# A chunked delta-rule recurrence on 64x64 squares in place of block-diagonal 128x128 matrices, with its vectors loaded early

## The chip, the cores and the metric

The kernel runs on one core of one Trainium2 chip. Its time is the device time in microseconds (us). TensorE (PE) multiplies and writes to PSUM; VectorE (DVE), ScalarE (ACT) and GpSimd (POOL) work beside it; SyncE (SP) issues most transfers. The four compute engines and SP run by themselves and wait for one another by semaphores. The kernel before took 2236.09 us (median of three runs, 2231.66 to 2236.36).

## The reference

The program is a two-layer block (retention, RG-LRU, two feed-forward layers), then a mixing layer over 256 context and 256 sequence tokens, then a product-key feed-forward layer. The change is in the mixing layer alone. What matters of it is its recurrence, of 4 heads with 64x64 states, in both directions of time, over 512 tokens:

```python
def step(S, inp):
    r_t, kk_t, v_t, w_t, b_t, k_t = inp
    sa = jnp.einsum('bhij,bhj->bhi', S, kk_t)
    S = S * w_t[:, :, None, :] - sa[..., None] * b_t[:, :, None, :] + v_t[..., None] * k_t[:, :, None, :]
    return S, jnp.einsum('bhij,bhj->bhi', S, r_t)
...
w_raw = w0 + jnp.einsum('btdr,drc->btdc', lw, w_up)          # tokens x 2 directions x 256 columns
decay = jnp.exp(-jnp.exp(-jax.nn.softplus(-w_raw) - 0.5))
a = jax.nn.sigmoid(a0 + jnp.einsum('btdr,drc->btdc', la, a_up))
kk = (k * k_k).reshape(B, T, RW_H, RW_DH)                    # then scaled to unit length
```

Beside it the layer has a neighbourhood attention of 8 heads (scores, a table of relative positions that is masked by column, softmax, output) and a short convolution; the three results go through one output projection.

## The kernel before, in words

The mixing layer first projects the tokens (`MIX_SLOTS`: seven slots of up to 512 columns of one weight matrix, each loaded by SP, split into a high part by ACT, L1076, and a low part by DVE, L1555, and multiplied in three products each, L2293 to L2295). `MIX_UNITS` says which piece of which slot goes to which tensor; slot 3 holds the gate and most of the attention's queries, slots 4 and 5 its keys and values and the convolution's columns, slot 6 the rest of the convolution.

After the last slot PE waits for vectors and low-rank weights (SP's loads at L887 to L896, issued behind a wait until slots 5 and 6 are used, since they lie in memory that those slots' parts occupied), computes eight `decay` units (L2572), DVE adds the bias (L1889), ACT takes the sigmoid (L1364), and DVE makes the scaled keys (L1892 to L1914). Only then does the recurrence start.

The recurrence works in chunks of 64 tokens, two to a tile of 128 rows, in four steps k with two directions d each: forward takes the tiles 0, 1, 2, 3, backward 1, 0, 3, 2. Each step makes cumulative decays (`cum`, L2663), scaled keys (L1975 to L1980), transposes (`tr`, L2674), products within the chunk (`ab`, and `l` where outputs are wanted, L2686), a product with v (`bv`, L2692), the inverse of a triangular matrix by five doublings (`lev`, L2697, then for n = 1 to 5 `t`, L2701, a transpose of the inverse so far; `y`, L2705, the level's part of A times it; `xy`, L2711, the product that is subtracted), `ug` (L2717), `mn` (L2725 to L2729: how the chunk maps a state), `rt` (L2740 to L2747) and, for each chunk, `st` (L2647 to L2656), which takes the state on. All are fp32. Each matrix is a 128x128 block for a pair of chunks or of heads, whose off-diagonal 64x64 quarters are zero, made so by masks on DVE (`MASK`, 16 masks of 128 columns). PSUM banks are evicted by ACT (`t`, `y`, `tr`, `ug`) and DVE (`xy`, `mn`, `lev`).

The order on all engines is one list, `RW_PLAN` (L254): the recurrence's units with d = 0 and d = 1 in turn, and at every 13th place a piece of an attention head (`ns` scores, `nt` a transposition, `no` output). Four PSUM banks go round (`unit`, L296); every engine works strictly in the order of its own instructions. POOL masks the attention's table (L1042), SP loads it (L881).

Within one unit, four products of 128x128 stand one behind another, for example `xy`:

```python
for j in range(4):
    ins = nc.tensor.matmul(quarter(j), TI[d][:, j // 2, j % 2, :], YY[d][:, j // 2, j % 2, :], start=True, stop=True)
```

Of the kernel before, what the change touches and what calls it, by code (L numbers as in the profile page):

```python
# [21 lines left out]
ALU = mybir.AluOpType  # L22
# [6 lines left out]
P = 128  # L29
D = 1024  # L30
# [14 lines left out]
def host_constants():  # L45
# [15 lines left out]
    same = a // 64 == b // 64  # L61
    for d in range(2):
        after = (lambda u, v: u > v) if d == 0 else (lambda u, v: u < v)
        for n in range(6):
            m = 1 << n

            out[f"level{d}{n}"] = ((a // (2 * m) == b // (2 * m)) & (a // m != b // m) & after(a, b)).astype(f4)
        out[f"strict{d}"] = (same & after(b, a)).astype(f4)
        out[f"incl{d}"] = (same & (after(b, a) | (a == b))).astype(f4)
    out["same"] = same.astype(f4)  # L70
# [6 lines left out]
    out["colok"] = ok.astype(f4)  # L77
# [122 lines left out]
def lru_size(kind, n):  # L200
# [7 lines left out]
MIX_SLOTS = [(1536, 512), (0, 512), (512, 512), (1024, 512), (2048, 512), (2560, 512), (3072, 384)]  # L208
# [11 lines left out]
    (3, [("t", 0, SEQ)], ("g", 0)), (3, [("t", 128, SEQ), ("t", 256, SEQ)], ("q", 0)), (3, [("t", 384, SEQ)], ("q", 2)),  # L220
    (4, [("t", 0, CTX), ("t", 0, SEQ)], ("nk", 3)),
    *[(4, [("n", t, 128, 384)], ("nv", t)) for t in range(4)],
    (5, [("n", t, 0, 128) for t in range(4)], ("nv3", 0)),
    (5, [("t", 128, SEQ), ("t", 256, SEQ)], ("z", 0)), (5, [("t", 384, SEQ)], ("z", 2)),
    (6, [("t", 0, SEQ), ("t", 128, SEQ)], ("z", 3)), (6, [("t", 256, SEQ)], ("z", 5)),
]


def rwkv_plan():


    st = lambda k, n: [(k, d, k ^ d, "st", n) for d in range(2)] if k >= 0 else []
    for k in range(4):
        work = ([("cum", 0), ("tr", 0), ("tr", 1), ("ab", 0), ("ab", 1)] + [("l", 0), ("l", 1)] * (k >= 2)
                + [("bv", 0), ("lev", 0)])
        for n in range(1, 6):
            work += [("t", n), ("y", n), ("xy", n)]
        work += [("ug", 0), ("mn", 0), ("mn", 1)] + [("rt", 0)] * (k >= 2)
        for what, n in work:
            for d in range(2):  # L240
                yield k, d, k ^ d, what, n
# [8 lines left out]
OTHER_WORK = {4: ("cv", 0), 6: ("cv", 1), 70: ("cv", 2), 72: ("rg", 0), 74: ("rg", 1)}  # L250
NO_UNIT = ("st", "nm", "nx", "no", "ny", "cv", "rg")
# [41 lines left out]
RB = 3  # L293

# [153 lines left out]
def first_and_second_block(nc, A, consts, out, mods, upto=99):  # L448
    cols = lambda name: consts[:, CONST_AT[name][0]:sum(CONST_AT[name])]
    with ExitStack() as ctx:  # L450
# [100 lines left out]
        CL = stage.take("context_lo", [P, KT, S], F32R)  # L551
        XC = stage.take("context", [P, TT, D])
        AB = stage.take("ada_bias", [P, 4, BANK])
        again = Region("split context", split_at, stage.end - split_at)
        WA = again.take("decay_and_a", [P, 4, 2, 2, 256])
        NP = Region("k, before", again.at, 8 * KB).take("scaled", [P, TT, D])
        KD = again.take("rw_k", [P, 4, 512])
        CKM = again.take("na_columns", [P, 2, 64])
        FLIP = again.take("na_flip", [P, P])
        GAIN = [XC[:, 0, :], Region("attention output, later", again.at, 4 * KB).take("gain", [P, D])[:, :]]  # L560
        NY = again.take("na_y", [P, TT, 512])
        RW2 = again.take("rw_y2", [P, TT, 256])
# [14 lines left out]
        AA = [ring.take(f"a_raw{d}", [P, 2, 2, P]) for d in range(2)]  # L577
        XX = [ring.take(f"inv_t{d}", [P, 2, 2, P]) for d in range(2)]
        TI = [ring.take(f"inv{d}", [P, 2, 2, P]) for d in range(2)]
        BT = [ring.take(f"b_t{d}", [P, 2, 2, P]) for d in range(2)]  # L580
        LL = [xs_again.take(f"l_t{d}", [P, 2, 2, 2, P]) for d in range(2)]
        AM = [scratch.take(f"a_level{d}", [P, 2, 2, P]) for d in range(2)]
        YY = [scratch.take(f"a_x{d}", [P, 2, 2, P]) for d in range(2)]
        NUG = [scratch.take(f"minus_u_g{d}", [P, 2, 4, 64]) for d in range(2)]
        hh_again = Region("idle input", hh_at, 8 * KB)
        MN = [hh_again.take(f"m_n{d}", [P, 2, 4, P]) for d in range(2)]
        EP = AM
        EN = YY
        RTt = [ring.take(f"r_turned{d}", [P, 2, P]) for d in range(2)]
        SB = [ring.take(f"state{d}", [P, 2, P]) for d in range(2)]  # L590
# [184 lines left out]
        def _(sp):  # L775
# [86 lines left out]

            for j, (c0, n) in enumerate(MIX_SLOTS):
# [3 lines left out]
                for h in range(2):  # L867
                    sp.dma_start(dst[:, 4 * h:4 * h + 4, :], W["w_in_2"][:, 4 * h:4 * h + 4, c0:c0 + n])\
                        .then_inc(s_wload[r], 16)
            deep(SLOTS["mix_out"], W["w_out_2"], 4)  # L870
            r, use = slot(SLOTS["mix_out"] + 1)
            sp.wait_ge(s_wlo[r], use)
            sp.dma_start(CKM[:, 0, :], cols("colok")).then_inc(s_bias, 16)
            sp.dma_start(CKM[:, 1, :], cols("colno")).then_inc(s_bias, 16)
# [8 lines left out]
            for j in range(2):  # L883
                r, use = slot(SLOTS["mix_in"] + 5 + j)
                sp.wait_ge(s_wused[r], use + 1)
            for n, (name, d) in enumerate([("rw_w0_2", 0), ("rw_a0_2", 0), ("rw_w0_2", 1), ("rw_a0_2", 1)]):
                sp.dma_start(RWR[:, n * 256:(n + 1) * 256], A[name][0, d].partition_broadcast(P)).then_inc(s_mix, 16)  # L887
            for n, name in enumerate(["rw_k_k_2", "rw_k_a_2", "rw_r_k_2", "rw_lnx_g_2"]):
                src = A[name][0].rearrange("h j -> (h j)") if name == "rw_r_k_2" else A[name][0]
                sp.dma_start(RWR[:, (4 + n) * 256:(5 + n) * 256], src.partition_broadcast(P)).then_inc(s_mix, 16)  # L890
            sp.dma_start(LORA[:, 0, :], A["rw_w_up_2"][0].rearrange("d r c -> (d r) c")).then_inc(s_mix, 16)
            sp.dma_start(LORA[:, 1, :], A["rw_a_up_2"][0].rearrange("d r c -> (d r) c")).then_inc(s_mix, 16)
            sp.dma_start(LORA[:, 2, :], A["rw_g_up_2"][0]).then_inc(s_mix, 16)
            sp.dma_start(chk, cols("chunk")).then_inc(s_mix, 16)
            sp.dma_start(prow[:, :], cols("same")).then_inc(s_mix, 16)
            sp.dma_start(MASK[:, :, :], consts[:, CONST_AT["level00"][0]:CONST_AT["same"][0]]  # L896
                         .rearrange("p (m n) -> p m n", n=P)).then_inc(s_mask, 16)
# [50 lines left out]
        def _(pool):  # L948
# [87 lines left out]
            for qt in range(TT):  # L1036
                if qt == 0:
                    pool.wait_ge(s_bias, 16 * 19)
                table = BIAS[:, qt, :, :].rearrange("p h (r c) -> p (h r) c", c=64)
                for j, op in enumerate((ALU.mult, ALU.add)):  # L1040
                    mask = CKM[:, j:j + 1, :].broadcast_to([P, 32, 64])
                    ins = nc.gpsimd.tensor_tensor(table, table, mask, op)  # L1042
                    if j == 0:
                        chain.done(ins)
# [1863 lines left out]
```

## Time and profile before

| | |
|---|---|
| median of three runs | 2236.09 us (2231.66 to 2236.36) |
| the profiled execution | 2229.75 us, span 2227.9 us |
| PE busy | 2033.6 us, 91% of the span |
| DVE busy | 1437.3 us, 65% |
| ACT busy | 1054.9 us, 47% |
| POOL busy | 407.8 us, 18% |
| granted TensorE clock, mean | 0.963 |
| stretch of the recurrence, 998 to 1283 us | PE busy 269.06 of 285 us, DVE 126.67, ACT 96.02 |

The busy share of PE is that of pipelined matmuls whose ends are modelled, so it is read beside the distance between their starts. In the trace an fp32 matmul shows as two records of a weight load (PEld) and two of a matmul (PE), an fp32 transpose as one of each. "128*64" in a row is the size of the part of the array that an instruction uses (rows * columns of weights), and the number behind it the size of what streams through.

### The profile page before, as it was taken

How to read it: one execution, taken by the hardware profiler on the slowest of the kernel's cores; microseconds unless marked ns; L12 is line 12 of the kernel's file. 1: busy time of each engine (PE TensorE's matmuls, PEld its weight loads, DVE VectorE, ACT ScalarE, POOL GpSimd, SP SyncE). 2: the span in 40 equal slices, each digit the busy share in tenths (PEclk: the TensorE clock that was granted, in tenths of full speed). 3: DMA queues.
4: the chain of work that ended last, by engine and by line, in shares of the span. 5: the costliest groups of instructions: out<-in, count | busy, mean ns of one | idle time of the engine just before them, and what ended most of it. 6: DMA issues, size and time to landing. Idle time of an engine off the chain costs nothing.

```text
span 2227.9 us, 36659 instructions
## 1 busy us (share of the span) xinstructions
PE 2033.6 (91%) x13383; PEld 1821.8 (82%) x13383; DVE 1437.3 (65%) x2240; ACT 1054.9 (47%) x2062; POOL 407.8 (18%) x333
## 2 busy tenths in 40 slices
PE   6998899987989999969999958988899999999996
PEld 6876788877888888958888848988899998777775
DVE  5536677767767664243544475888799995666665
ACT  4343444357654444323333343444477775555554
POOL 2101000001000000030000000777766672000000
PEclk9999999998999999978999979999999999999998
DMA  7552466744457863220000163555544444555553
GB/s 257 189 189 85 166 234 221 249 161 142 170 189 235 270 232 134 85 68 1 1 1 1 39 151 81 152 156 155 170 140 139 139 143 165 190 190 189 188 188 132
DMA packets 212850, 333.64 MB, mean 150 GB/s; under 512 B 23654, under 2 KB 141148, under 8 KB 212584
## 3 DMA queue, kind: packets, MB, share of 16 engines
q1 hardware_dynamic: 209320, 321.20, 44.9%
q0 software_dynamic: 3392, 10.52, 1.3%
q8 instruction: 96, 1.57, 0.3%
q14 instruction: 42, 0.34, 0.0%
HBM read 330.58 MB, written 1.08 MB: 149 GB/s over the span
## 4 chain that ended last, share of the span: by engine, by line
PE 65%; DVE 13%; PEld 7%; DMA 5%; issue 4%; ACT 3%; SPq 2%; PEldq 1%; DVEq 0%; POOL 0%; ACTq 0%
PE psum L2293 17%; PE psum L2295 16%; PE psum L2294 16%; DMA u_rows<-in_peer_u_dram 3%; PE psum L2865 3%; PEld psum L2293 2%; PEld psum L2294 2%; PEld psum L2295 2%; DVE u_turned L2196 2%; PE psum L2705 2%; DVE weights_lo L1555 2%; PE psum L2711 2%; SPq L921 2%; PE psum L2686 1%; ACT weights_hi L1076 1%
## 5 line engine op out<-in xcount | busy, mean ns | idle before, releaser
L1555 DVE TENSOR_TENSOR weights_lo<-weights,weights_hi 128x1024 fp32r<-128x1024 f32 (+2 forms) x336 | 345.5, 1086 | 261.7 <-ACT weights_hi L1076 256.4
L2293 PE MATMUL psum<-input_hi,weights_hi 128*128 128x256 f32 x1288 | 371.3, 288 | 14.5 <-issue 5.3
L1076 ACT ACTIVATE weights_hi<-weights 128x1024 fp32r<-128x1024 f32 (+2 forms) x336 | 289.3, 931 | 178.6 <-PEq L2340 118.6
L1055 POOL TENSOR_TENSOR u_lo<-u_turned,u_hi 128x512 fp32r<-128x512 f32 x256 | 329.9, 1311 | 217.2 <-ACT u_hi L1452 217.2
L2294 PE MATMUL psum<-input_lo,weights_hi 128*128 128x256 f32 x1288 | 367.3, 285 | 0.0
L2295 PE MATMUL psum<-input_hi,weights_lo 128*128 128x256 f32 x1288 | 367.0, 285 | 0.0
L2293 PE MATMUL psum<-input_hi,u_hi 128*128 128x256 f32 x1024 | 298.8, 292 | 14.0 <-POOL u_lo L1055 13.0
L2294 PE MATMUL psum<-input_lo,u_hi 128*128 128x256 f32 x1024 | 292.1, 285 | 0.0
L2295 PE MATMUL psum<-input_hi,u_lo 128*128 128x256 f32 x1024 | 292.0, 285 | 0.0
L2293 PEld LDWEIGHTS psum<-input_hi,weights_hi 128*128 128x128 f32 x1288 | 249.8, 194 | 29.8 <-issue 28.0
L2294 PEld LDWEIGHTS psum<-input_lo,weights_hi 128*128 128x128 f32 x1288 | 249.9, 194 | 0.0
L2295 PEld LDWEIGHTS psum<-input_hi,weights_lo 128*128 128x128 f32 x1288 | 249.7, 194 | 0.0
L2293 PEld LDWEIGHTS psum<-input_hi,u_hi 128*128 128x128 f32 x1024 | 198.3, 194 | 16.5 <-issue 11.1
L2293 PE MATMUL psum<-v_hi,act_hi 128*128 128x512 f32 x512 | 203.7, 398 | 0.0
L2295 PE MATMUL psum<-v_hi,act_lo 128*128 128x512 f32 x512 | 200.5, 392 | 0.0
L2294 PE MATMUL psum<-v_lo,act_hi 128*128 128x512 f32 x512 | 200.0, 391 | 0.0
L2294 PEld LDWEIGHTS psum<-input_lo,u_hi 128*128 128x128 f32 x1024 | 198.7, 194 | 0.0
L2295 PEld LDWEIGHTS psum<-input_hi,u_lo 128*128 128x128 f32 x1024 | 198.4, 194 | 0.0
L2196 DVE STREAM_TRANSPOSE u_turned<-u_rows 128x1024 f32<-128x1024 f32 x128 | 157.9, 1236 | 38.5 <-DMA u_rows<-in_peer_u_dram 33.6
L1452 ACT ACTIVATE u_hi<-u_turned 128x512 fp32r<-128x512 f32 x256 | 147.1, 627 | 12.2 <-DVE u_turned L2196 12.1
L2267 DVE TENSOR_TENSOR act_lo<-act_table,act_hi 128x256 fp32r<-128x256 f32 x128 | 54.5, 425 | 133.6 <-ACT act_hi L1527 133.6
L1527 ACT ACTIVATE act_hi<-act_table 128x256 fp32r (+1 forms) x128 | 53.5, 418 | 166.3 <-PE psum L2295 166.0
(387 smaller groups left out, 3927.6 us busy)
## 6 DMA issues: line engine op xcount, KB each, us to landing
u_rows<-in_peer_u_dram SPq DMA_DIRECT2D x512, 128.0 KB, 2.7
weights<-in_ffn_w_in_dram SPq DMA_DIRECT2D x44, 1024.0 KB, 7.5
v_rows_even<-in_peer_v_dram SPq DMA_DIRECT2D x64, 512.0 KB, 3.3
v_rows_odd<-in_peer_v_dram SPq DMA_DIRECT2D x64, 512.0 KB, 3.3
weights<-in_ret_w_in_dram SPq DMA_DIRECT2D x24, 1024.0 KB, 7.3
ada_rows_in<-in_ada_w_dram SPq DMA_DIRECT2D x24, 1024.0 KB, 5.4
weights<-in_ffn_w_out_dram SPq DMA_DIRECT2D x44, 512.0 KB, 6.6
weights<-in_lru_w_in_dram SPq DMA_DIRECT2D x12, 1024.0 KB, 6.2
```

What stands on the lines that cost most here:

```text
L921: sp.dma_start(UR[32 * a:32 * a + 32, b, :].rearrange("p (c k) -> p c k", c=4), columns.rearrange("(c e) k -> e c k", c=4)).then_inc(s_ur[ ...
L1055: nc.gpsimd.tensor_tensor(UTL[:, b, half, :], turned[:, half, :], UTH[:, b, half, :].bitcast(F32), ALU.subtract).then_inc(s_ul[b], 1)
L1076: nc.scalar.activation(whi[:, r, at_], wraw[:, r, at_], ACT.Copy).then_inc(s_whi[r], 1)
L1452: nc.scalar.activation(UTH[:, b, half, :], turned[:, half, :], ACT.Copy).then_inc(s_uh[b], 1)
L1527: nc.scalar.activation(AH[:, j % 2:j % 2 + 1, :], GT[:, bass.ds(4 * i + j, 1), :], ACT.Copy)\
L1555: ins = nc.vector.tensor_tensor(wlo[:, r, at_], wraw[:, r, at_], whi[:, r, at_].bitcast(F32), ALU.subtract)
L2196: nc.vector.transpose(UT[j % 4].rearrange("p k (c e) -> p c k e", c=4), UR[:, b, :].rearrange("p (c k j) -> p c k j", c=4, k=KT)).then_inc ...
L2267: nc.vector.tensor_tensor(AL[:, b:b + 1, :], GT[:, bass.ds(4 * i + j, 1), :], AH[:, b:b + 1, :].bitcast(F32), ALU.subtract).then_inc(s_as, 1)
L2293: nc.tensor.matmul(o, ah, bh, start=start, stop=False)
L2294: nc.tensor.matmul(o, ah, bl, start=False, stop=False)
L2295: return nc.tensor.matmul(o, al, bh, start=False, stop=stop)
L2865: ins = nc.tensor.matmul(PS[:, 4 + g % 4, x * P:(x + 1) * P], ONE[:, g % 2, 1, x, :], ONE[:, g % 2, 0, x, :], start=True, stop=True)
```

## The change

**Squares.** Matrices are kept as 64x64 squares, two in a tile (one on partitions 0 to 63, one on 64 to 127). Each 128x128 product becomes two of 64x64, one in the upper left and one in the lower right quarter of the array, in turn (`halves()`); `ab`, `l`, `mn` and `rt` use the other two quarters as well, and put their two halves into two banks (`PAIRED`). Evictions are 256 wide in place of 512, and masks 64 wide; the mask on `mn` is gone and its eviction goes from DVE to ACT. The transposes `lev` and `t` become products with a 64x64 identity, since they lie in quarters. `st` no longer adds the old state and the chunk's part on PE; DVE does it (two operations before, and a fused one after, PE's product).

**Vectors early.** SP loads the vectors behind slot 3 of 7, into other memory; the slots are reordered so that the `decay` units come after slot 5, before slot 6; DVE makes its first three key operations before them. The masks (a table of 1600 columns in place of 2048) are loaded by POOL's queue once slot 5 is used.

**One bias addition.** The attention's table was multiplied by one mask and added to another, on POOL; now DVE adds one mask, at places 4 and 30 of the plan. The convolution moves from places 4 and 6 to 50 and 60.

```diff
-MIX_SLOTS = [(1536, 512), (0, 512), (512, 512), (1024, 512), (2048, 512), (2560, 512), (3072, 384)]
+MIX_SLOTS = [(1536, 512), (0, 512), (512, 512), (2048, 512), (2560, 512), (1024, 512), (3072, 384)]
+DECAY_SLOT = 5
+MIX_VECTORS = 12
...
-OTHER_WORK = {4: ("cv", 0), 6: ("cv", 1), 70: ("cv", 2), 72: ("rg", 0), 74: ("rg", 1)}
+OTHER_WORK = {4: ("bm", 0), 30: ("bm", 1), 50: ("cv", 0), 60: ("cv", 1), 70: ("cv", 2), 72: ("rg", 0), 74: ("rg", 1)}
...
+                halves = lambda: ((j, slice(64 * c, 64 * c + 64)) for j in range(4) for c in range(2))
...
                 elif what == "t":
                     evacuated(U("xy", n - 1) if n > 1 else U("lev"))
-                    for j in range(4):
-                        ins = nc.tensor.transpose(quarter(j), XX[d][:, j // 2, j % 2, :], ident[:, :])
+                    for j, ch_ in halves():
+                        ins = nc.tensor.matmul(PS[ch_, b, j * 64:j * 64 + 64], XX[d][ch_, j // 2, j % 2, :],
+                                               SQM[ch_, 16, :], start=True, stop=True)
...
                 elif what == "xy":
                     evacuated(U("t", n))
                     evacuated(U("y", n))
-                    for j in range(4):
-                        ins = nc.tensor.matmul(quarter(j), TI[d][:, j // 2, j % 2, :], YY[d][:, j // 2, j % 2, :],
-                                               start=True, stop=True)
+                    for j, ch_ in halves():
+                        ins = nc.tensor.matmul(PS[ch_, b, j * 64:j * 64 + 64], TI[d][ch_, j // 2, j % 2, :],
+                                               YY[d][ch_, j // 2, j % 2, :], start=True, stop=True)
...
                     if (k, n) != (3, 1):
                         for hp in range(2):
-                            o = PS[:, 5 + d, hp * P:(hp + 1) * P]
-                            nc.tensor.matmul(o, ident[:, :], SB[d][:, hp, :], start=hp == 0, stop=False,
-                                             skip_group_check=True)
-                            nc.tensor.matmul(o, ident[:, :], MN[d][:, c, 2 + hp, :], start=False, stop=False,
-                                             skip_group_check=True)
-                            ins = nc.tensor.matmul(o, MN[d][:, c, hp, :], SB[d][:, hp, :], start=False, stop=hp == 1,
-                                                   skip_group_check=True)
+                            for par in range(2):
+                                half = slice(64 * par, 64 * par + 64)
+                                ins = nc.tensor.matmul(PS[half, 5 + d, hp * 64:hp * 64 + 64], MN[d][half, c, hp, :],
+                                                       SB[d][half, n, hp, :], start=True, stop=True)
```

On PE, inside the third and fourth doubling of step 0, the kernel before has these instructions (`inv_t` is the inverse so far, transposed; `a_level` the level's part of A; 93 and 94 are directions 0 and 1):

```order
L2701 MATMUL psum<-ident,inv_t0_93 128x128 x4
L2701 MATMUL psum<-ident,inv_t1_94 128x128 x4
L2601 MATMUL psum<-ident,na_scores_117 128x128 x4
L2705 MATMUL psum<-inv_t0_93,a_level0_101 128x128 x4
L2705 MATMUL psum<-inv_t1_94,a_level1_102 128x128 x4
L2711 MATMUL psum<-a_x0_103,inv0_95 128x128 x4
L2613 MATMUL psum<-na_v_58,na_probs_t_118 128x64 x4
L2711 MATMUL psum<-a_x1_104,inv1_96 128x128 x4
```

The changed kernel has, at the same place:

```order
L2755 MATMUL psum<-masks_78,inv_t0_95 64x64 x8
L2755 MATMUL psum<-masks_78,inv_t1_96 64x64 x8
L2648 MATMUL psum<-ident,na_scores_119 128x128 x4
L2760 MATMUL psum<-inv_t0_95,a_level0_101 64x64 x8
L2760 MATMUL psum<-inv_t1_96,a_level1_102 64x64 x8
L2766 MATMUL psum<-a_x0_103,inv0_97 64x64 x8
L2660 MATMUL psum<-na_v_58,na_probs_t_120 128x64 x4
L2766 MATMUL psum<-a_x1_104,inv1_98 64x64 x8
```

The order of the units is the same; each has eight squares in place of four full matrices, and the attention's pieces between them are unchanged and use the full array.

On DVE, between the last weight split and the first scaled keys of the recurrence (`bv_kappa0`), the kernel before has:

```order
L1555 TENSOR_TENSOR weights_lo<-weights,weights_hi 128x768 x4
L1889 TENSOR_TENSOR decay_and_a_68<-psum,rw_rows_80 128x512 x8
L1892 TENSOR_TENSOR rw_kk_81<-z_k_51,rw_rows_80 128x1024
L1895 TENSOR_TENSOR turned0_78<-rw_kk_81 128x1024
L1896 TENSOR_REDUCE small<-turned0_78 128x16
L1899 MEMSET state0_111 128x256
L1899 MEMSET state1_112 128x256
L1905 SCALAR_TENSOR_TENSOR rw_k_70<-decay_and_a_68,rw_rows_80 128x4x256
```

and the changed kernel:

```order
L1571 TENSOR_TENSOR weights_lo<-weights,weights_hi 128x768 x4
L1903 TENSOR_TENSOR rw_kk_73<-z_k_51,rw_rows_70 128x1024
L1906 TENSOR_TENSOR rw_k_76<-rw_kk_73 128x1024
L1907 TENSOR_REDUCE small<-rw_k_76 128x16
L1912 TENSOR_TENSOR decay_and_a_68<-psum,rw_rows_70 128x512 x8
L1917 SCALAR_TENSOR_TENSOR rw_k_76<-decay_and_a_68,rw_rows_70 128x4x256
```

The three key operations stand ahead of the eight bias additions, and the clearing of the states (now with that of `r_turned`, 512 wide) has moved behind the whole chain.

## Rows read from the trace of the kernel before

**Rows 1.** Busy by stretch, the recurrence: PE, PEld, DVE, ACT, clock, DMA share, GB/s.

```profile
998.00:1283.00 285.00, 269.06 (x1984) 235.91 (x1983) 126.67 (x244) 96.02 (x200) 0.95 0.02 8
```

**Rows 2.** The chain of waits before the recurrence: start, us, what.

```profile
968.82 5.52 DMA param_rows<-tables_dram
974.38 3.66 PE psum L2572 x15
978.07 3.68 DVE decay_and_a L1889 x6
...
996.76 2.11 PE psum L2674 x8
```

**Rows 3.** Timeline of ACT, 953 to 984: start, us, engine, line, operation.

```profile
953.50 0.39 ACT L1317 ACTIVATE sc_z<-psum 128x256 f32<-128x256 f32 x1 [2.28 <-PE psum L2295]
...
962.62 0.38 ACT L1317 ACTIVATE sc_z<-psum 128x256 f32<-128x256 f32 x1 [2.28 <-PE psum L2295]
...
982.43 1.28 ACT L1366 ACT_TABLE_LOAD   x1
```

**Rows 4.** Timeline of DVE at the same place.

```profile
993.00 2.48 DVE L1914 TENSOR_TENSOR decay_and_a<-decay_and_a,rw_kk 128x1024 f32<-128x1024 f32 x2
995.52 0.43 DVE L1975 TENSOR_TENSOR bv_kappa<-rw_kk,a_level 128x256 f32<-128x256 f32 x1
```

**Rows 5.** Groups by form, 1000 to 1290: busy us, mean ns, idle before.

```profile
L2705 PE MATMUL psum<-inv_t,a_level 128*128 128x128 f32 x320 | 44.9, 295 | 4.3 <-DVE a_level L2000 3.7 <-ACTq L1379 0.6
...
L2004 DVE TENSOR_TENSOR inv_t<-inv_t,psum 128x512 f32<-128x512 f32 x40 | 27.5, 688 | 61.8 <-PE psum L2711 61.8
...
L2686 PE MATMUL psum<-turned 64*128 64x128 f32 x192 | 25.2, 305 | 1.2 <-ACTq L1379 0.6 <-ACT turned L1317 0.5
...
L1317 ACT ACTIVATE a_x<-psum 128x512 f32<-128x512 f32 x40 | 23.9, 597 | 25.2 <-PE psum L2705 25.2
...
L2725 PE MATMUL psum<-beta,minus_u_g 64*128 64x128 f32 x64 | 12.7, 288 | 0.0
...
L2652 PE MATMUL psum<-state,ident 128*128 128x128 f32 x56 | 11.5, 287 | 0.0
...
L1985 DVE TENSOR_TENSOR b_t<-psum,masks 128x256 f32<-128x256 f32 x16 | 6.8, 425 | 15.7 <-ACT a_raw L1401 15.4
...
L1401 ACT ACTIVATE a_raw<-psum 128x256 f32<-128x256 f32 x16 | 6.1, 383 | 18.5 <-PE psum L2686 18.3
```

**Rows 6.** Timeline of PE, the doublings of step 2.

```profile
1153.78 0.60 PE L2701 MATMUL psum<-ident,inv_t 128*128 128x128 f32 x4
...
1174.72 0.63 PE L2701 MATMUL psum<-ident,inv_t 128*128 128x128 f32 x4
...
1176.21 2.02 PE L2705 MATMUL psum<-inv_t,a_level 128*128 128x128 f32 x16
...
1187.92 2.02 PE L2717 MATMUL psum<-bv_kappa,inv_t 128*128 128x128 f32 x16
```

**Rows 7.** Timeline of PE from 1274.2: products in two column halves in turn, others behind.

```profile
1274.21 0.66 PE L2747 MATMUL psum<-l_t,minus_u_g 128*64 128x128 f32 x8
1274.70 0.60 PE L2647 MATMUL psum<-state,r_turned 128*64 128x128 f32 x4
1275.23 0.49 PE L2652 MATMUL psum<-state,ident 128*128 128x128 f32 x2
```

**Rows 8.** Timeline of PEld, the weight loads of the first of these.

```profile
1274.21 0.42 PEld L2747 LDWEIGHTS psum<-l_t,minus_u_g 128*64 128x64 f32 x8
```

**Rows 9.** Line L2747, 1274.15 to 1274.24: count, ns min/median/max, first and last start.

```profile
L2747 PE MATMUL psum<-l_t,minus_u_g x2: 323/323/323, 1274.2 to 1274.2; 128*64 128x128 f32 x2
```

**Rows 10.** Stretches of 4 us: PE, PEld, DVE, ACT, POOL busy, then granted clock.

```profile
976.00:980.00 4.00, 4.00 (x27) 3.62 (x24) 3.22 (x6) 2.43 (x5) 0.00 (x0) 0.78 0.00 0
...
1000.00:1004.00 4.00, 4.00 (x17) 3.79 (x18) 0.82 (x2) 0.82 (x3) 0.00 (x0) 0.50 0.00 0
...
1008.00:1012.00 4.00, 4.00 (x20) 3.78 (x19) 1.45 (x3) 1.44 (x4) 0.00 (x0) 0.50 0.00 0
1020.00:1024.00 4.00, 4.00 (x29) 4.00 (x28) 0.00 (x0) 1.63 (x3) 0.00 (x0) 0.73 0.00 0
```

More of the change, by code:

```diff
@@ L237, in rwkv_plan @@
             work += [("t", n), ("y", n), ("xy", n)]
-        work += [("ug", 0), ("mn", 0), ("mn", 1)] + [("rt", 0)] * (k >= 2)
+        work += [("ug", 0), ("mn", 0)] + [("rt", 0)] * (k >= 2)
         for what, n in work:
             for d in range(2):
-                yield k, d, k ^ d, what, n
+                for half in range(2 if what in PAIRED else 1):
+                    yield k, d, k ^ d, what, n + half
             if what in ("cum", "tr") and (what, n) != ("tr", 1):
@@ L882, in _ @@
                         .then_inc(s_bias, 16)
[L883 to L897, printed above, removed]
             sp.wait_ge(s_nx, NA_STEPS)
@@ L1035, in _ @@
             stored(11)
[L1036 to L1044, printed above, removed]
-                ins.then_inc(s_biasm, 1)
+            r, use = slot(SLOTS["mix_in"] + DECAY_SLOT)
+            pool.wait_ge(s_wused[r], use + 1)
+            pool.dma_start(MALL[:, :], consts[:, CONST_AT["strict0"][0]:CONST_AT["chunk"][0]]).then_inc(s_mask, 16)
             evacuated(UNITS["rw_out"])
@@ L1359, in _ @@
                     at_unit += 1
-            for u in range(8):
-                t, d = divmod(u, 2)
-                evacuated(UNITS["decay"] + u)
-                nc.scalar.activation(WA[:, t, d], WA[:, t, d], ACT.Sigmoid).then_inc(s_sig, 1)
             act.wait_ge(s_kk, 1)
@@ L1417, in _ @@
                     ins.then_inc(s_free[b], 1)
+                elif what == "mn":
+                    if k and n == 0:
+                        act.wait_ge(s_st[d], 2 * k + 1)
+                    out_of(u, MN[d][:, n, :, :].rearrange("p a b -> p (a b)"), src=first(256))
             for tt in range(TT):
@@ new lines, in _ @@
+                        ins.then_inc(s_stp[d], 1)
+                    if k >= 2:
+                        for h in range(4):
+                            o = (t - SEQ) * 256 + h * 64
+                            nc.tensor.matmul(PS[ch_, 4, o:o + 64], RTt[d][:, h // 2, h % 2, ch_], SB[d][:, n, h // 2, :],
+                                             start=False, stop=False, skip_group_check=True)
+                    continue
+                if what in PAIRED and n == 0:
+                    continue
@@ L2661, in _ @@
+                if what in PAIRED:
+                    both = [free_bank(U(what, half)) for half in range(2)]
+                else:
+                    b = free_bank(U(what, n))
                 if what == "cum":
-                    for j, m in enumerate((7, 6)):
-                        ins = nc.tensor.matmul(PS[:, b, j * 256:(j + 1) * 256], MASK[:, 8 * d + m, :], WA[:, t, d, 0, :],
+                    for j, m in enumerate((1, 0)):
+                        ins = nc.tensor.matmul(PS[:, b, j * 256:(j + 1) * 256], MASK[:, 2 * d + m, :], WA[:, t, d, 0, :],
@@ L2715, in _ @@
                     evacuated(U("bv"))
[L2716 to L2718 removed]
+                    for h, ch_ in halves():
+                        ins = nc.tensor.matmul(PS[ch_, b, h * P:(h + 1) * P], XX[d][ch_, h % 2, h // 2, :],
+                                               BK[d][ch_, :, h, :], start=True, stop=True)
```

366 lines of the change are left out of this document (215 added, 151 removed).

## The prediction

> **What bounds the kernel now.** I read the busy time by stretch first, since the change touches one stage. From 998 to 1283 us, 285 of the 2227.9, PE is busy 269.06 us while DVE has 126.67 and ACT 96.02 [rows 1]: the recurrence goes at PE's pace, nearly. The chain of waits says the same and shows the second place. Ahead of the recurrence PE stands until a transfer lands at 974.34, then makes the `decay` units, and DVE works alone until the first transposes at 996.76 [rows 2]; its last two preparations begin at 993.00 and its first scaled key at 995.52 [rows 4]. The groups by form say what a unit costs outside PE: an eviction of 512 columns takes DVE 688 ns and ACT 597, one of 256 columns 425 and 383 [rows 5]. The timeline gives PE's pace: 16 records of `y` take 2.02 us, less about 0.28 for the last one's run through the array, so 0.115 a record; a transpose unit of four takes 0.63 less 0.27 [rows 6]. I use 0.112 a record, so 0.90 for a `y` or `xy` unit (8 records), 0.45 for a `t` unit (4).
>
> **The vectors early.** The last columns of slot 5 are evicted at 953.50, those of slot 6 at 962.62 [rows 3]: slot 6 is 9.1 us of PE. In the changed kernel the `decay` units can start at 953.3. DVE adds their biases at 3.68/6 = 0.61 us each [rows 2], eight are 4.9 us, and PE goes on to slot 6 at about 958.2, done 967.3. ACT's square root stands behind slot 6's evictions in ACT's order, with a table load of 1.28 [rows 3]: 969.3. DVE has done the four key operations by then, but waits for that root; the reciprocal, one scaling (1.24, half of the pair's 2.48) and the pair (2.48) [rows 4] bring it to 973.4, and four clears, about 0.5 each, to 975.3. So the first scaled key comes at 975.3 in place of 995.52: 20 us less. SP's twelve loads, some 0.5 us each, stand ahead of the loads of slots 4 to 6, which wait for DVE's splits; the masks through POOL's queue have from 953 to 970. I give both nothing; if the vectors delayed a slot it would be their 6 us.
>
> **Do quarters run side by side?** All else hangs on it. No square of 64x64 is in this trace, but `rt` has products on 128*64 halves in turn. Eight of its records take 0.66 us, so 0.39 between the first start and the last [rows 7]; two start at once [rows 9], and four pairs at 0.11 us make up the eight. The eight weight loads take 0.42 less 0.137, also paired [rows 8]. One half alone (L2647, always the same half) takes 0.60 for four, 0.11 a record [rows 7]. So halves run in parallel, each at its own 0.11 for 128 columns. For 64 columns of weights and 64 streamed, half of that: 0.056 a pair, 16 records of a square unit in 0.45 us. The bounds: 0.39 us for 16 instructions (loads and matmuls) is 24 ns each; if that is a floor of issue, a square unit is 32 x 24 ns = 0.78. If quarters don't pair it is 0.90. I take 0.45, since the pairs of rows 9 are no slower than one half alone.
>
> **The levels.** With directions interleaved, the loop is t1, y0, y1, xy0, xy1, DVE, t1. Before: 0.45 + 4 x 0.90, 0.16 for the last record's end, 0.69 on DVE and 0.25 of hand-overs (my estimate) = 5.15. The five levels of step 2 run from 1153.78 to 1187.92, 34.1 us [rows 6], so 8.4 of them are the attention's. After: y1's result must also pass ACT before xy1, as PE no longer hides it: 0.45 (t1) + 0.90 (y0, y1) + 0.2 + 0.1 + 0.38 (ACT) + 0.1 + 0.66 (xy1 with its end) + 0.1 + 0.42 (DVE) + 0.15 = 3.45. Five levels: 17.3 against 25.7, so 8.4 less; four steps, 34 less. PE now idles 3.45 - 6 x 0.45 = 0.75 a level, in which attention pieces fit: I count half of it for 20 levels, 7 less. `t` and `lev` gain nothing on PE: 16 square records in place of 4 transposes, 0.45 both.
>
> **The rest of a step.** By records in rows 5 at 0.112: `ab` and `l` 192, 21.5 us, to 12 units of 0.45 to 0.9 on four quarters, 8 (-13); `mn` three lines of 64, 21.5, to 8 x 1.35 (-11); `st` three lines of 56, 18.8, to 14 x 0.22 (-16). With `bv` and `rt` (-3 each, by the same halving) this is 46 less on PE. Between `cum` and `lev`, evictions of 512 columns and DVE's scaled keys stay as they are and come to light, so I count 0.7 of it: 32 less. In `st` DVE gets two small operations more, before it waits for PE.
>
> **What the change adds.** Each change of array form costs: from the last L2647 start (1274.70 + 0.60 - 0.27 = 1275.03) to L2652 at 1275.23 it is 0.20 in place of 0.11 [rows 7], so 0.09. Counting forms in the instruction order gives 71 changes before and 127 after: +5. The two additions of the attention's mask on DVE, 2048 columns, cost 2.5 each by the 1.24 per 1024 [rows 4], one between transposes and one in a level: +3 of 5. With a thinner PE the clock drops more often between bursts: +5, from the 4 us stretches at 0.5 in rows 10.
>
> The Trainium skill bears on it. TensorEngine Tiling (Array Packing), Key Properties, says that a change of the tiling mode drains TensorE; rows 7 agree, with 0.09 us.
>
> **Sum.** -20 - 34 - 7 - 32 + 5 + 3 + 5 = -80. From the profiled execution's 2229.75 that is 2150; it lies 6 us under the median, so I say 2153.
>
> **Rivals.**
>
> *The clock stays at its lower level (slower).* At 1000 to 1012 us PE is busy 4.00 of 4.00 us and the granted clock is 0.50, 1.2 of 2.4 GHz [rows 10]; what ran were 64*128 products (L2686), scores of 64 rows and `bv`. It rose within 1020 to 1024, when `y` ran on the full array. At 976 to 980 it also rose (0.78), with `decay` units on both row halves in turn. Squares in two quarters use half of the array. If they can't raise the clock, then once it has fallen in the 8 us gap before the first transposes it stays down. PE's work before is about 240 us: 1984 records [rows 1] at 0.112 make 222, and the few that stream 256 or 512 columns some 18 more. After it is 36 (the halved `y` and `xy`) and 46 less, 158 at the full clock and 316 at half; with 12 us of form changes and 15 of waits 343, against 285: +58, less 20 for the vectors: 2268, range 2240 to 2300. From 2150 to 2268 is 118 us, so the result turns slower once about two thirds of the recurrence's work is done at 0.5. For it: 12 us of busy PE without a rise. Against it: rows of both halves are active, as with the `decay` units, and transposes become products. The Trainium skill (TensorE: Matmul & The Clock Gate, Part 1: The HAM clock gate) sets the clock by how busy PE has been, with no word of the part of the array in use; by that rule squares would hold the clock and this rival falls, but the stretch from 1000 to 1012 in rows 10 does not bear the rule out.
>
> *Quarters don't pair, or issue is the floor.* A unit is 0.78 to 0.90, `t` twice as dear as before. The loop is then about 4.9, 0.25 less a level (-5), and the rest gains only in `st` (-14): with the vectors and what is added 2229.75 - 20 - 5 - 14 + 13 = 2204, up to 2225. Against it: rows 7 to 9.
>
> *The early vectors do nothing*, because DVE's chain waits for slot 6 anyway: then 2173. The order on DVE speaks against it: only the root waits for slot 6.
>
> **Chances.** Forecast 0.55 (own range 2110 to 2190, the third rival's 2173 with it), quarters unpaired or issue-bound 0.13, clock low 0.29, others 0.03. The range that leaves out 2 in 10 cuts the low clock's upper half and a little below: 2108 to 2272. This kernel's runs tell 0.2% (4.5 us) from no change. Faster: 0.55 + 0.13 + a little of the low clock, 0.69; slower 0.27; the same 0.04.
>
> **What would show it.** The first scaled key near 975; square units of 16 records in about 0.45 plus 0.27 us, two records starting at once; a level without attention pieces near 3.5 us; the recurrence some 205 us long; granted clock above 0.85 in it. The forecast is wrong if the clock's mean there is under 0.75, if a square record takes over 0.045, or if ACT or DVE work without gaps while PE waits, which their 96 and 127 us of 285 don't let expect.

## The result, and the profile after

The changed kernel takes 2144.1 us (median of 4, 2142.4 to 2147.2) against 2235.4: ratio 0.960, 95% interval 0.958 to 0.961. Its profiled execution spans 2140.6 us, 87.3 less than the span of before. I split that at two points, the first transposes ahead of the recurrence and the transposes of the attention's output behind it. Two rows cut at them, first of before, then of after; columns as in [rows 1], with POOL's busy time ahead of the clock:

```profile
996.80:1280.50 283.70, 268.33 (x1976) 235.31 (x1976) 125.48 (x245) 94.34 (x196) 0.00 (x0) 0.94 0.02 8
```

```profile
980.40:1195.60 215.20, 188.43 (x3777) 151.62 (x3778) 96.15 (x271) 82.14 (x212) 0.00 (x0) 0.96 0.04 12
```

The recurrence is 68.5 us shorter, what lies ahead of it 16.4, what lies behind 2.4. PE is busy 79.9 us less and idles 27 in place of 15. DVE and ACT lose 29 and 12 us of work, by the narrower operations and, on DVE, because the eviction of `mn` went to ACT.

The preparation, DVE's and ACT's timelines of after, which answer to [rows 3, 4]:

```profile
958.31 4.88 DVE L1912 TENSOR_TENSOR decay_and_a<-psum,rw_rows 128x512 f32<-128x512 f32 x8 [5.11 <-PE psum L2583]
...
972.93 0.25 DVE L1922 RECIPROCAL small<-small 128x16 f32<-128x16 f32 x1 [4.04 <-ACT small L1380]
...
974.48 2.48 DVE L1926 TENSOR_TENSOR decay_and_a<-decay_and_a,rw_kk 128x1024 f32<-128x1024 f32 x2
...
979.14 0.42 DVE L2003 TENSOR_TENSOR bv_kappa<-rw_kk,a_level 128x256 f32<-128x256 f32 x1 [0.23 <-DVE r_turned L1932]
```

```profile
956.85 0.38 ACT L1331 ACTIVATE na_q<-psum 128x256 f32<-128x256 f32 x1 [2.28 <-PE psum L2330]
...
970.83 0.38 ACT L1331 ACTIVATE sc_z<-psum 128x256 f32<-128x256 f32 x1 [2.28 <-PE psum L2330]
971.23 1.28 ACT L1380 ACT_TABLE_LOAD   x1
```

The chain is the one forecast: additions, four key operations, a wait of 4.04 us for the root (behind slot 6's evictions and a table load), reciprocal, scaling, pair, clears, first scaled key at 979.14.

A part of step 2's levels on PE (L2755 `t`, L2760 `y`, L2766 `xy`), answering to [rows 6]:

```profile
1103.03 1.48 PE L2755 MATMUL psum<-masks,inv_t 64*64 64x64 f32 x32
1104.88 1.15 PE L2760 MATMUL psum<-inv_t,a_level 64*64 64x64 f32 x32 [0.37 <-ACTq L1393]
1106.19 1.15 PE L2766 MATMUL psum<-a_x,inv 64*64 64x64 f32 x32 [0.17 <-ACT a_x L1331]
1107.27 0.66 PE L2648 MATMUL psum<-ident,na_scores 128*128 128x128 f32 x4
1107.86 1.15 PE L2755 MATMUL psum<-masks,inv_t 64*64 64x64 f32 x32
...
1113.99 1.15 PE L2755 MATMUL psum<-masks,inv_t 64*64 64x64 f32 x32
...
1116.41 0.68 PE L2760 MATMUL psum<-inv_t,a_level 64*64 64x64 f32 x16 [0.80 <-ACTq L1393]
...
1118.24 0.68 PE L2755 MATMUL psum<-masks,inv_t 64*64 64x64 f32 x16
...
1129.21 1.05 PE L2772 MATMUL psum<-bv_kappa,inv_t 64*64 64x128 f32 x15
```

Two units of one kind, 32 records, take 1.15 less 0.22 for the last one's run: 0.465 a unit, where `y` took 0.90. The five levels run from 1103.03 to 1129.21, 26.2 us for 34.1. `[0.80 <-ACTq L1393]` is PE waiting for a bank until ACT has read the attention's scores in it. The waits by releaser, from 980 to 1196:

```profile
PE psum L2736 <- ACTq L1393: 2.7, 2, 1.7
...
PE psum L2766 <- ACTq L1393: 2.3, 4, 0.7
PE psum L2760 <- ACTq L1393: 2.1, 4, 0.8
```

With the smaller ones these waits for L1393 are 10.0 us; in the kernel before, where the line is L1379, they were 1.6. And the clock, to be read beside [rows 10]:

```profile
972.00:976.00 4.00, 4.00 (x31) 3.87 (x32) 2.97 (x4) 2.30 (x4) 0.00 (x0) 0.95 0.00 0
976.00:996.00 20.00, 15.21 (x165) 10.77 (x163) 10.75 (x26) 6.02 (x16) 0.00 (x0) 0.50 0.00 1
996.00:1000.00 4.00, 4.00 (x58) 3.55 (x55) 0.39 (x2) 1.87 (x5) 0.00 (x0) 0.57 0.02 4
1000.00:1004.00 4.00, 3.85 (x59) 2.84 (x58) 1.18 (x3) 0.64 (x2) 0.00 (x0) 1.00 0.00 0
```

It falls before the recurrence, comes back among the first levels' squares and stays up: of the rival of the low clock some 20 us are seen here.

### The profile page after: what moved, and what is told of

Same layout as the page of the kernel before. It is cut to its first block, busy times and chain, and to the rows that moved or that the text cites. A ratio compares the mean times of both kernels' runs of the same rounds, so it can differ in the third digit from the quotient of the medians.

```text
span 2140.6 us, 40342 instructions
## 1 busy us (share of the span) xinstructions
PE 1955.3 (91%) x15183; PEld 1738.9 (81%) x15183; DVE 1408.8 (66%) x2268; ACT 1042.2 (49%) x2078; POOL 390.9 (18%) x330
## 4 chain that ended last, share of the span: by engine, by line
PE 69%; DVE 13%; DMA 4%; ACT 4%; issue 4%; PEld 2%; SPq 2%; PEldq 0%; POOL 0%; DVEq 0%; ACTq 0%
PE psum L2328 20%; PE psum L2329 19%; PE psum L2330 19%; PE psum L2931 3%; DVE u_turned L2231 2%; DMA u_rows<-in_peer_u_dram 2%; DVE weights_lo L1571 2%; SPq L942 1%; PE psum L2766 1%; PE psum L2755 1%; ACT weights_hi L1090 1%; PE psum L2760 1%; PE psum L2638 1%; PEld psum L2328 1%; PEld psum L2329 1%
## 5 line engine op out<-in xcount | busy, mean ns | idle before, releaser
L2328 PEld LDWEIGHTS psum<-input_hi,weights_hi 128*128 128x128 f32 x1288 | 250.6, 195 | 29.6 <-issue 27.8
```

Of the source, the lines that this page charges most:

```text
L2328: nc.tensor.matmul(o, ah, bh, start=start, stop=False)
```

## The experiments

Times are medians, compared with the 2144.1 of the changed kernel; each run stands beside runs of the kernel before on its chip, which gave 2232.7 to 2234.6, and 2235.4 beside the changed kernel; so up to 2.7 us of a difference may be the chip's. A difference under some 4 us is not told from none. "Levels" is the time from a step's first `t` to its `ug` on PE; of after 29.4, 26.7, 26.2 and 25.1, of before 36.1, 36.0, 34.1 and 32.7. The last step's levels, first of before, then of after:

```profile
1229.80:1262.50 32.70, 31.23 (x242) 27.62 (x241) 15.40 (x26) 14.45 (x26) 0.00 (x0) 1.00 0.18 65
```

```profile
1158.50:1183.60 25.10, 23.66 (x518) 19.43 (x513) 9.43 (x25) 10.30 (x26) 0.00 (x0) 1.00 0.24 86
```

**Quarters one after the other (e1_unpaired).**

```diff
-halves = lambda: ((j, ...) for j in range(4) for c in range(2))      # lev, t, y, xy
+one_half_first = lambda: ((j, ...) for c in range(2) for j in range(4))
```

> The changed kernel (2144.1 us) with the order inside the units lev, t, y and xy changed: the eight products of one quarter come first, then the eight of the other, so that neighbouring records are in the same quarter. Theory (two quarters side by side give the gain of the levels): a unit of 16 records goes from 0.46 us to 0.90 between its first start and its end, 120 units in 20 levels and 8 lev units, +0.45 each = 58 us, of which the idle time in the levels (some 8 us) hides a part: about +50 us, 2194. Rival (the quarters do not matter, the instruction's issue or the smaller tile alone sets 0.028 us a record): nothing changes, 2144 within 5.

2173.7 us, +29.6: between the two. The second theory is out, the size of the first was wrong. A pair of units and a step's levels of this kernel:

```profile
1141.95 1.54 PE L2767 MATMUL psum<-a_x,inv 64*64 64x64 f32 x32
```

```profile
1050.00:1081.40 31.40, 30.46 (x531) 26.28 (x526) 12.92 (x30) 10.22 (x27) 0.00 (x0) 1.00 0.01 2
```

1.54 less 0.22 is 1.32 for two units, 0.66 each and not 0.90. Even in this order the quarters overlap in part, at the change within a unit and at the seam to the next. The four steps' levels took 128.9 us against 107.4: 21.5 of the 29.6, of which some 2.5 are the clock's (0.90 and 0.95 in steps 2 and 3).

**The seams closed too (e7_seams).**

```diff
+... for c in ((0, 1) if d == 0 else (1, 0)) for j in range(4)
```

> As e1_unpaired, but direction 1 begins each unit with the quarter with which direction 0 ended, so that at the seam between two units as well neighbours are in the same quarter. Theory (in e1_unpaired the second half of a unit ran beside the first half of the next one, so two units took 24 x 0.056 = 1.36 us in place of 0.92; with the seams closed two take 1.8): each of the 128 units of lev, t, y and xy costs 0.45 us more than in the changed kernel, 58 us, less about 8 hidden: +50, 2194. Rival (what e1_unpaired lost is not the overlap but something else, such as the drops of the clock seen in it): as e1_unpaired, 2174.

2193.0 us (five runs, 2192.1 to 2218.4), +48.9. The number is the theory's, its composition is not:

```profile
1228.20 1.70 PE L2756 MATMUL psum<-masks,inv_t 64*64 64x64 f32 x32
```

```profile
994.50:1051.50 57.00, 57.00 (x526) 50.33 (x525) 11.20 (x24) 10.79 (x27) 0.00 (x0) 0.50 0.01 2
1079.00:1134.60 55.60, 55.60 (x521) 49.38 (x520) 12.91 (x30) 10.19 (x26) 0.00 (x0) 0.50 0.00 1
1164.90:1197.10 32.20, 30.86 (x517) 27.40 (x516) 8.58 (x22) 10.93 (x28) 0.00 (x0) 1.00 0.01 3
1228.20:1259.10 30.90, 30.46 (x517) 27.26 (x516) 9.39 (x24) 10.20 (x26) 0.00 (x0) 1.00 0.19 70
```

At the full clock two units take 1.70 less 0.22, 0.74 each (so the change within a unit still overlaps some), and a step's levels 32.2 and 30.9, 6 us over after: 24 for four steps. What remains of the 49 I put to the clock: its mean over the other four runs is 0.951 to 0.952, where those of after have 0.962 to 0.966, and 0.012 of 2190 us is 26. In this profile, that of the execution of 2218.4 us, steps 0 and 1 ran their levels wholly at 0.50, with PE busy 57.00 of 57.00 and 55.60 of 55.60 us. In after, whose squares go in pairs, the clock came back within 996 to 1000. So the rival of the low clock was no fancy: it came true here for two steps of four. That the missing pairs are the reason is not shown: the same squares kept 1.00 in steps 2 and 3.

**Quarters of the same rows (e5_rows).**

```diff
-for j: for x in range(2): for par in range(2):       # ab, l
+for par, j in (...): for x in range(2):              # one row half first; mn likewise
```

> The changed kernel with the order inside ab, l and mn changed: all products of one row half come first, alternating between the two column halves, then the other row half. Theory (quarters that share rows but not columns also run side by side, so four at once become two at once): a unit of 32 records goes from 0.46 to 0.90 us, one of 48 from 0.67 to 1.35; 12 x 0.45 + 8 x 0.67 = 11 us, partly beside the waits for ACT there: +8, 2152. Rival (quarters of the same rows run one after the other): 1.8 and 2.7 us a unit, +32, 2176.

2151.2 us, +7.1, near the theory's 8, but not shown to be the theory's: the profiled recurrence has a granted clock of 0.90, and the one execution with a mean clock of 0.966 took 2144.0 us. What the order does is read from a unit. One `ab` unit of this kernel and of after:

```profile
1041.61 0.98 PE L2735 MATMUL psum<-turned 64*64 64x64 f32 x32
```

```profile
1040.97 0.69 PE L2736 MATMUL psum<-turned 64*64 64x64 f32 x32
```

Less the last run, 0.76 against 0.47 us: slower than four at once, and faster than the 1.8 of one after the other. In after 32 records start in 0.47 us, 15 ns each with as many weight loads beside them: the prediction's 24 ns an instruction is no floor.

**The vectors late again (e2_late), and only the place of the decay units (e2b_behind_slot6).**

```diff
-if j == 3: load_mix_vectors()         # e2_late: after slots 5 and 6 are used
-DECAY_SLOT = 5                        # both
+DECAY_SLOT = 6
-(key operations) (additions)          # e2_late
+(additions) (key operations)
```

> The changed kernel with the vectors late again: SP loads them after slots 5 and 6 are used, the decay units stand behind slot 6 on PE, ACT and DVE, and DVE's three key operations behind the additions. Theory: the first scaled key comes near 995 in place of 979.14, +16 us, 2160. Rival (the new order of the slots or fewer clears made the gain, the vectors' time being hidden): at most +5 us, 2149.

> The changed kernel with only the place of the decay units changed, behind slot 6 in place of slot 5; loads and key operations stay early. Theory: slot 6 ends at 966 in place of 970.8, the eight units' additions end at 971.2, then DVE's four operations (5.0), reciprocal, scaling and pair (4.1) and clears (2.1) bring the first scaled key to 982.8 in place of 979.14: +4 us, 2148; so 12 of the 16 us would be the early loads. Rival (slot 6 covers the whole of the decay work): +9 us or more, 2153.

e2_late: 2161.9, +17.8, with the first scaled key at 998.49; the theory. e2b: 2149.0, +4.9 (its runs lie between 2142.9 and 2154.8), with the key at 984.01. DVE's timeline of both, in this order:

```profile
978.05 1.29 DVE L1906 TENSOR_TENSOR decay_and_a<-psum,rw_rows 128x512 f32<-128x512 f32 x2 [29.12 <-PE psum L2585]
...
998.49 0.42 DVE L2005 TENSOR_TENSOR bv_kappa<-rw_kk,a_level 128x256 f32<-128x256 f32 x1 [0.23 <-DVE r_turned L1934]
```

```profile
967.19 4.87 DVE L1912 TENSOR_TENSOR decay_and_a<-psum,rw_rows 128x512 f32<-128x512 f32 x8 [14.23 <-PE psum L2583]
...
984.01 0.42 DVE L2003 TENSOR_TENSOR bv_kappa<-rw_kk,a_level 128x256 f32<-128x256 f32 x1 [0.23 <-DVE r_turned L1932]
```

So of 19.4 us between 979.14 and 998.49 the early loads and key operations are 14.5 and the place ahead of slot 6 is 4.9.

**Root, clears and chunk unit (e3_prelude).** ACT's square root ahead of the sigmoids, the four clears on POOL, the chunk unit behind the first `tr`.

> The changed kernel with three moves before the recurrence: the root of the norms ahead of the sigmoids on ACT (in place of behind slot 6's evictions), the four clears on POOL in place of DVE, and PE's chunk unit behind the first transposes in place of ahead of the first cum. Theory (DVE's wait for the root, 4.04 us, and the clears, 2.1 us, stand on the path, and cum on PE behind chunk just beside it): the first scaled key at 974 in place of 979.14, -5 us, 2139. Rival (the clock drops in that stretch anyway, or the clears on POOL end later than DVE needs): 0 within 2 us.

2148.1 us, +4.0: no gain, though the first part came true (the first scaled key, then the chunk unit on PE):

```profile
973.55 0.42 DVE L2009 TENSOR_TENSOR bv_kappa<-rw_kk,a_level 128x256 f32<-128x256 f32 x1
```

```profile
976.70 3.63 PE L2711 MATMUL psum<-small,decay_and_a 128*128 128x2 f32 x32
```

5.6 us won, 3.63 given back, as the 32 thin records now stand on the recurrence's own path. That leaves a gain of 2, and yet the recurrence ended at 1197.0 (after: 1195.6), at a granted clock of 0.95 over 222.2 us in place of 0.96 over 215.2, which is 2.5 us more lost; the last us has no place.

**The same, with the thin records in PE's waits (e8_spread).**

```diff
+CHUNK_WORK = {2: (0, 6), 10: (6, 10), 11: (10, 13), 13: (13, 16)}    # item: products
```

> As e3_prelude (root early on ACT, clears on POOL), but PE's 32 thin chunk records (3.6 us) are cut in four pieces of 1.4, 0.9, 0.7 and 0.7 us, put where PE waits in the first step: behind the first cum, ahead of both bv and ahead of the second lev. Theory (in e3_prelude the first scaled key came 5.5 us earlier and the chunk unit on the path took 3.6 of it back): the recurrence ends 5 us earlier than in the changed kernel, 2139. Rival (the granted clock in the stretch decides, and an earlier start meets as many drops as before): 2144 to 2148.

2133.8 us (2132.4 to 2140.0), -10.3, ratio to before 0.956 (0.954 to 0.958): this version beats both, by 8.7 us if the two ratios to before are compared. PE and the clock:

```profile
972.05 1.40 PE L2683 MATMUL psum<-small,decay_and_a 128*128 128x2 f32 x12
973.75 0.41 PE L2731 MATMUL psum<-ident,bv_kappa 128*128 128x128 f32 x2 [0.30 <-DVE k_rel L2015]
```

```profile
974.00:978.00 4.00, 3.00 (x46) 1.88 (x44) 3.11 (x4) 2.19 (x6) 0.00 (x0) 1.00 0.00 0
...
986.00:990.00 4.00, 3.85 (x97) 3.58 (x92) 1.09 (x3) 1.41 (x4) 0.00 (x0) 1.00 0.02 4
```

The first `t` came at 984.4 in place of 995.0: 6.6 us by the earlier start, the other 4 as the clock did not fall between 966 and 1006. Of these 10.6 the recurrence's end kept 7.4 (1188.2). The profile is of the execution of 2140.0 us, and what lies behind the recurrence took 950.0 us in it against 945.0: its span is only 2.4 us under that of after. The size of the gain rests on the medians, its place on this profile.

**Full products between the thin ones (e10_wide).**

```diff
+if hp == 0:
+    nc.tensor.matmul(PS[:, b, P:2 * P], WA[:, t, d, 0, 0:P], ident[:, :], ...)   # 128 columns, never read
```

> The changed kernel with eight more products, 128 columns each on the full array and never read, set between the 16 two-column products of the chunk unit ahead of the recurrence: 1.8 us more PE work there. Theory (the clock falls at 974 to 976 in the changed kernel because PE streams almost nothing in those two-column products, and then stays at half until 998): the granted clock stays at 1.00 over 974 to 998, which gives back 5 to 8 us of the recurrence: 2138. Rival (it falls in PE's wait ahead of the first transposes in any case): the clock is 0.5 from about 980 as before, and the extra products cost what they delay the first cum by, 0 to 2 us: 2144 to 2146.

2147.8 us, +3.7: the theory falls.

```profile
970.00:974.00 4.00, 3.53 (x31) 3.56 (x31) 1.84 (x3) 3.24 (x4) 0.00 (x0) 0.96 0.00 0
974.00:978.00 4.00, 4.00 (x20) 4.00 (x20) 3.31 (x6) 0.07 (x1) 0.00 (x0) 0.50 0.00 0
...
982.00:986.00 4.00, 2.74 (x45) 2.15 (x46) 3.30 (x4) 2.06 (x6) 0.00 (x0) 1.00 0.00 0
...
994.00:998.00 4.00, 4.00 (x66) 3.55 (x65) 1.09 (x3) 1.49 (x4) 0.00 (x0) 0.55 0.02 4
```

The clock fell about 2 us earlier than in after, came back sooner and fell again. So it falls here with full products between the thin ones too; why e8_spread was spared is open.

**The way of y through ACT (e9_pieces).**

```diff
-out_of(u, YY[d][...], src=first(256))
+for q in range(4): nc.scalar.activation(YY[d][:, q // 2, q % 2, :], PS[:, b, q * 64:q * 64 + 64], ACT.Copy)
```

> The changed kernel with ACT's eviction of y in four pieces of 64 columns in place of one of 256: some 0.45 us longer, 40 times. Theory (the levels are still held by PE, whose squares and attention fill most of a level; ACT's part counts only in the levels without attention): +2 to +4 us, 2147. Rival (after the change the path through ACT and DVE sets the level): 20 levels x 0.45 for the second direction's y alone = +9, up to +18 for both: 2153 to 2162.

2153.8 us, +9.7: the rival's number. But the levels alone don't show 9: 29.8, 27.4, 27.7 and 25.9 are 3.4 us over after, while the whole recurrence went from 215.2 to 221.8 at a clock of 0.94. PE's waits for y's eviction say the same: 4.0 us in 13 waits of `xy`, where after has 0.5 in 3. So I take it that this way comes onto the path once ACT is 0.45 us slower, for some 3 us; in the changed kernel itself it is hardly on it. The rest of the 9.7 the runs don't place.

**Attention pieces elsewhere (e4_apart, e11_places).**

```diff
-NA_WORK = (..., ("nt", 7), ("no", 10))      # e4_apart
+NA_WORK = (..., ("nt", 7), ("no", 14))
+at = [place[k, 0, "xy", n]] * 2 + [place[k, 1, "xy", n], place[k, 1, *turn], place[k, 0, *out_]]   # e11_places, on e8_spread
```

> The changed kernel with the attention's output products (1.1 us of PE) moved four places later, from 10 to 14 behind their scores, that is right behind the next head's scores. Theory (the new waits for ACT's exponential of the scores, 10 us on PE, come because too little PE work stands between the scores and the fourth unit that reuses their bank): a third to a half of them goes, -4 us, 2140. Rival (PE waits elsewhere instead, since the output products filled another gap): 0 or up to +4 us.

> As e8_spread, with the attention's pieces tied to places of the recurrence in place of every 13 items: one head in the first part of each step, three in its levels 1, 3 and 5, each head's scores ahead of direction 0's xy (where PE waits for ACT's y), its exponential next on ACT, its transposes ahead of direction 1's t, its output products ahead of the next xy. Theory (e9_pieces showed that the way of y through ACT is on the path, and PE's new waits for the scores' exponential come from banks asked back too soon): the waits for ACT in the levels go, 6 us of the 10 for the exponential and some of y's, 2127. Rival (levels 2 and 4, left without pieces, idle 0.75 us each as forecast, and the clock drops more often): 2134 to 2142.

e4_apart: 2152.2, +8.1. Its waits for L1393 are 9.6 us against 10.0, so nothing was relieved. Its recurrence, cut at the same two points as the first rows above, has the clock at 0.93 where after has 0.96, some 7 of its 8.2 us more:

```profile
980.30:1203.70 223.40, 193.85 (x3776) 157.07 (x3777) 96.04 (x271) 82.14 (x212) 0.00 (x0) 0.93 0.03 12
```

e11_places: 2142.2, 8.4 slower than e8_spread. The waits for the exponential fell to 5.9 us, and another took their place, 6.3 us for the subtraction of `xy` on DVE. In the one below, the scores' maximum (0.69 us from 1047.00) and two operations of other work behind it (L1975, L1976, 0.7 us each) stood ahead of that subtraction (L2051, at 1049.24):

```profile
1046.89 1.15 PE L2783 MATMUL psum<-a_x,inv 64*64 64x64 f32 x32
1049.81 0.68 PE L2772 MATMUL psum<-masks,inv_t 64*64 64x64 f32 x16 [1.76 <-DVE inv_t L2051]
```

**The mask additions on POOL (e6_pool).** The two operations of `bm` moved to POOL's program, behind the masks' load.

> The changed kernel with the two additions of the attention's mask on POOL, in its order where the kernel before had them, in place of DVE. Theory (DVE has room for both, 2.28 us each): 0 within 2 us, 2144. Rival (they delay ab's evictions and a level): -3 us, 2141.

2142.6 us (2136.5 to 2148.6), -1.5: no difference that the runs can tell. The profile, of the execution of 2148.6 us, has a trade in it, DVE's row first, then POOL's:

```profile
975.04 6.67 DVE L1932 TENSOR_TENSOR decay_and_a<-decay_and_a,rw_kk 128x1024 f32<-128x1024 f32 x2
```

```profile
969.40 9.97 POOL L1064 TENSOR_TENSOR na_bias<-na_bias,na_columns 128x2048 f32<-128x2048 f32 x2 [11.53 <-DMA na_bias<-in_na_rpb_dram]
```

Beside POOL's additions DVE's pair took 6.67 us in place of 2.48, and the first scaled key came at 983.90, 4.8 late; the recurrence took 216.8. On DVE an addition costs 2.28 us, and DVE idles 1.57 us behind the first.

## Why the prediction was right, point by point

The forecast, 2153, was 9 us over the measured 2144.1, well within its own range. On the spans of the profiled executions -80 was said and -87.3 came.

- *Vectors early, -20.* The first scaled key came at 979.14, 16.4 earlier. The working holds: each operation stands where it was put. The clock is what it left out. At the layer's first evictions after was already 3.3 us later than before (852.76 against 849.44), with a granted clock of 0.96 from 800 to 890 where before had 1.00; 975.3 + 3.3 is 978.6. e2_late prices the part by itself at +17.8, so the rival "the early vectors do nothing" falls. That SP's loads delay no slot holds too: slot 5's last eviction is at 956.22 with late loads, 956.85 with early ones, and the layer's first was 0.6 us apart already.
- *Square units in 0.45 us.* 0.465. e1_unpaired, e7_seams and e5_rows show that it is the pairing, of quarters with and without common rows. The rival "quarters don't pair, or issue is the floor" is refuted, by 0.47 us for 32 records, 15 ns each, where the bound took 24 ns an instruction.
- *The levels, -34 and -7.* From 138.9 us (sum of before) to 107.4, -31.5. This is the term that was mis-sized, by 10 us. A level without a piece of attention takes 4.2 us (1113.99 to 1118.24, and 1064.95 to 1069.13), not 3.45, and in before it took 5.7, not 5.15, from the row below to the one at 1174.72 in [rows 6]:

```profile
1168.98 1.04 PE L2701 MATMUL psum<-ident,inv_t 128*128 128x128 f32 x8
```

The difference, 1.5, is close to the forecast 1.7; the two sizes are not. What did not come is the half level of idle time that was to take attention pieces, the 7: PE idles 7.8 us in the 20 levels of after and 8.2 in those of before. The pieces bring waits of their own (10 us for the exponential, of which 4.4 at `y` and `xy`). y's way through ACT, which the forecast put on the path, shows in 0.5 us of waits in all.
- *The rest of a step, -32.* With the form changes, mask additions and the clock the rest went from 144.8 to 107.8, -37. Of this the clock has 5 (below), which leaves -32 where -32 + 5 + 3 = -24 was said. The wide evictions between `cum` and `lev` did come to light (waits for DVE's scaled keys, `b_t` and `l_t`), for less than the three tenths that I gave them. And `mn` gave more than said: a unit of 48 records takes 0.75 us (1133.58 to 1134.33), where 1.35 was counted, about 5 us in eight units.
- *Form changes, +5.* From the last L2766 start (1106.19 + 1.15 - 0.22 = 1107.12) to L2648 at 1107.27 is 0.15 in place of 0.06: 0.09 each, as said. The Trainium skill (TensorEngine Tiling (Array Packing), Key Properties) has the drain at a change of mode; the trace agrees, with that price.
- *Mask additions, +3.* No cost is seen. DVE idles 1.57 us behind the first; e6_pool, -1.5, can't size the term, since it is within the noise and brings a later first key of its own.
- *The clock, +5.* The sign was wrong. At a granted mean of 0.94 over 283.7 us, 17 us of full-speed work were lost, at 0.96 over 215.2 us 8.6: 8 us won, 4 of them in the levels (from the clocks of their rows), 13 from what was said. So without the clock the levels gave 28 of the 41 said and the rest 8 more than said; the clock made up the difference, and nothing in the profile of before promised that. That the total came so near is in this part luck.
- *The rival of the low clock.* Given 0.29, and it deserved a place. The clock did not fall in a gap as it said: in after it went from 1.00 to 0.50 at about 975.6, with PE busy 4.00 of 4.00 us from 972 to 976. It then came back among squares in pairs, which the rival had as doubtful. In e7_seams it did not come back for the length of two steps' levels, and even there a kernel of 2192 to 2218 us stays under the one before. Why it comes back in one and not in the other stays open. The Trainium skill (TensorE: Matmul & The Clock Gate, Part 1: The HAM clock gate) goes by how busy PE has been; 57.00 of 57.00 us busy at 0.50 in e7_seams speaks against that as the whole rule.
- *The signs.* The recurrence took 215.2 us. The "some 205" among the signs does not follow from the sum, whose terms without the vectors are -60, so 225 from the 285 of before.

## What to carry to other kernels

Small matrices in the quarters of the array pay by how they are ordered: neighbours in the instruction stream should lie in different quarters, and the order alone moved the time by 30 to 49 us here, of which 19 to 24 are the levels at the full clock. When the main engine gets thinner, look next at work that is thin but long (32 two-column products, 3.6 us): moving it whole gave nothing, and filling the waits with it, beside the same earlier first key, gave some 9 to 10 us. And where an engine's clock moves by itself, price a change by the rows at equal clock first, and trust a difference of a few us only when timed runs and rows agree.

## What was not expected of the hardware

The clock does not follow from the program alone. After and e1_unpaired issue the same instructions on PE until `lev`. In after the stretch 986 to 990 is at 0.50 and the clock is back at about 999.4 (0.57 over 996 to 1000); in e1_unpaired it fell 1.6 us sooner and was back within 982 to 986:

```profile
974.00:978.00 4.00, 4.00 (x14) 3.51 (x14) 3.45 (x6) 0.75 (x3) 0.00 (x0) 0.50 0.00 0
...
982.00:986.00 4.00, 3.80 (x42) 2.32 (x40) 1.64 (x2) 1.69 (x5) 0.00 (x0) 0.73 0.00 0
986.00:990.00 4.00, 2.33 (x74) 2.04 (x75) 2.10 (x7) 1.79 (x6) 0.00 (x0) 1.00 0.02 4
```

Quarters overlap also without strict alternation: eight records of one quarter followed by eight of another take 0.66 to 0.74 us, where one after the other would be 0.90 and in turn 0.47. And POOL and DVE slow each other: an addition of 2048 columns takes 4.5 us on POOL in the kernel before and 5.0 beside DVE's pair in e6_pool, against 2.28 on DVE, and it stretches that pair 2.7 times (6.67 us against 2.48).
